# Squares added by VectorE, gate units first, selection rounds gathered in the first attention, layers written out

## The reference, cut to what matters

```python
def swiglu(x, w_gate, w_up, w_down):
    return (jax.nn.silu(x @ w_gate) * (x @ w_up)) @ w_down
...
    x = x + 0.5 * swiglu(rmsnorm(x, ffn1_norm), ffn1_w_gate, ffn1_w_up, ffn1_w_down)
    h = rmsnorm(x, mix_norm) @ w_in
    ...
    o_a = chunk_relpos_attention(hd4(a_q, A_HEADS), hd4(a_k, A_HEADS), hd4(a_v, A_HEADS), a_rel_bias)
    o_b = dsa_attention(rope(hd4(b_q, B_HEADS), pos), rope(hd4(b_k, B_HEADS), pos), hd4(b_v, B_HEADS),
                        rope(hd4(i_q, IDX_HEADS), pos), rope(i_k[:, :, None, :], pos)[:, :, 0, :], i_w)
    o_c = mla_attention(c_q, c_kv, c_kr, c_q_norm, c_kv_norm, c_w_uq, c_w_ukv, pos)
    x = x + jnp.concatenate([o_a, o_b, o_c], axis=-1) @ w_out
    x = x + 0.5 * swiglu(rmsnorm(x, ffn2_norm), ffn2_w_gate, ffn2_w_up, ffn2_w_down)
```

```python
        gates = jax.nn.sigmoid(proj("gates").reshape(b, s, N_BRANCH, D_MODEL) + b_gate[l])
        projected = jnp.einsum('bsnc,ncd->bsnd', branches, w_branch[l])
        mixed = jnp.sum(gates * projected, axis=2)
        x = x + mixed @ w_out[l]
        ...
        x = x + (jax.nn.silu(gate_pre) * val) @ w_down[l]
```

## Time and profile before

| | us |
|---|---|
| median of 3 runs (lowest, highest) | 4180.34 (4179.41, 4185.32) |
| profiled execution, its span | 4181.7, 4180.1 |
| PE busy | 3886.0 (93%) |
| DVE busy | 1864.2 (45%) |
| ACT busy | 1487.7 (36%) |
| POOL busy | 427.1 (10%) |
| granted clock, mean | 0.961 |

### The profile page before, as it was taken

One profiled execution on the slowest core, in us unless ns is written; L12 is line 12 of the kernel. 1 busy time (PEld: TensorE's weight loads), 2 busy tenths in 40 slices (PEclk: granted clock), 3 DMA queues, 4 the chain that ended last, 5 costly groups with the idle time before them and its releaser, 6 DMA issues.

```text
span 4180.1 us, 50030 instructions
## 1 busy us (share of the span) xinstructions
PE 3886.0 (93%) x17196; PEld 3048.2 (73%) x17196; DVE 1864.2 (45%) x3059; ACT 1487.7 (36%) x2433; POOL 427.1 (10%) x414
## 2 busy tenths in 40 slices
PE   7999997789999999987899998899999999898999
PEld 6887664578878887664678886777776668577887
DVE  3433457644434433467544344335542224634652
ACT  3222343432223223333432234436534453523221
POOL 1100001111001100011011021101100000101110
PEclk9999998899999999998899999999999999999999
DMA  3332221023323323211123333131122203222333
GB/s 107 95 98 98 81 61 46 10 82 97 96 91 91 95 95 116 61 43 39 43 85 96 106 116 87 43 84 46 46 76 55 62 22 92 74 80 80 96 92 99
DMA packets 484466, 322.07 MB, mean 77 GB/s; under 512 B 10929, under 2 KB 464177, under 8 KB 483281
## 3 DMA queue, kind: packets, MB, share of 16 engines
q1 hardware_dynamic: 479760, 303.91, 24.8%
q0 software_dynamic: 3392, 14.03, 1.0%
q10 hardware_dynamic: 1152, 2.10, 0.1%
HBM read 310.82 MB, written 8.52 MB: 76 GB/s over the span
## 4 chain that ended last, share of the span: by engine, by line
PE 65%; issue 19%; DVE 5%; ACT 4%; DVEq 3%; POOL 2%; POOLq 2%; ACTq 0%; DMA 0%; SPq 0%
PE bank L233 18%; PE bank L235 18%; PE bank L234 18%; ACT w_hi L218 2%; PE bank L2115 1%; PE bank L2121 1%; DVEq L2427 1%; POOLq L396 1%; PE bank L2135 1%; DVEq L2441 1%; PE bank L2124 1%; DVE s_ring L2432 1%; PE bank L974 1%; PE bank L1172 1%; PE bank L1199 1%
## 5 line engine op out<-in xcount | busy, mean ns | idle before, releaser
L233 PE MATMUL bank<-h_hi,w_hi 128*128 128x512 f32 x3064 | 1234.6, 403 | 63.3 <-DVE h_lo L386 35.5
L225 DVE TENSOR_TENSOR w_lo<-w_raw,w_hi 128x1024 fp32r<-128x1024 f32 (+1 forms) x571 | 741.0, 1299 | 1118.1 <-ACT w_hi L218 1113.4
L235 PE MATMUL bank<-h_lo,w_hi 128*128 128x512 f32 x3128 | 1230.3, 393 | 0.0
L234 PE MATMUL bank<-h_hi,w_lo 128*128 128x512 f32 x3064 | 1205.5, 393 | 0.0
L218 ACT ACTIVATE w_hi<-w_raw 128x1024 fp32r<-128x1024 f32 (+1 forms) x571 | 591.8, 1038 | 581.0 <-DMA w_raw<-in_ffn_w_down 316.0
L233 PEld LDWEIGHTS bank<-h_hi,w_hi 128*128 128x128 f32 x3064 | 580.6, 189 | 232.9 <-issue 47.5
L235 PEld LDWEIGHTS bank<-h_lo,w_hi 128*128 128x128 f32 x3128 | 591.1, 189 | 130.3 <-issue 2.5
L234 PEld LDWEIGHTS bank<-h_hi,w_lo 128*128 128x128 f32 x3064 | 580.5, 189 | 115.1 <-issue 2.7
L233 PE MATMUL bank<-g_hi,w_hi 128*128 (+1 forms) x880 | 342.7, 389 | 2.9 <-DVE gu_ring L2443 2.9
L235 PE MATMUL bank<-g_lo,w_hi 128*128 (+1 forms) x880 | 342.6, 389 | 0.0
L234 PE MATMUL bank<-g_hi,w_lo 128*128 (+1 forms) x880 | 342.6, 389 | 0.0
(11 more groups left out here) (428 smaller groups left out, 4549.7 us busy)
## 6 DMA issues: line engine op xcount, KB each, us to landing
w_raw<-in_w_in SPq DMA_DIRECT2D x105, 512.0 KB, 3.8
w_raw<-in_ffn_w_gate SPq DMA_DIRECT2D x88, 512.0 KB, 3.8
w_raw<-in_ffn_w_up SPq DMA_DIRECT2D x88, 512.0 KB, 3.8
w_raw<-in_ffn_w_down SPq DMA_DIRECT2D x88, 512.0 KB, 3.4
w_raw<-in_w_mix SPq DMA_DIRECT2D x50, 512.0 KB, 4.0
w_raw<-in_w_up SPq DMA_DIRECT2D x44, 512.0 KB, 3.8
w_raw<-in_w_branch SPq DMA_DIRECT2D x32, 512.0 KB, 4.1
w_raw<-in_w_down SPq DMA_DIRECT2D x22, 512.0 KB, 3.4
```

The lines of the kernel that those rows point to most:

```text
L225: dve.tensor_tensor(WL[:, slot(c), 0:w], RAW[:, slot(c), 0:w], WH[:, slot(c), 0:w].bitcast(F32), ALU.subtract).then_inc(w_lo, 1)
L233: pe.matmul(bank, wh, xh, start=start, stop=False)
L234: pe.matmul(bank, wl, xh, start=False, stop=False)
L235: return pe.matmul(bank, wh, xl, start=False, stop=stop)
```

## The change

Four edits. In an FFN, the squares go to eight tiles of their own (`SQUARES`; four of them are tiles of rings that are not yet in use then), DVE adds them instead of POOL, between its two weight splits, ACT splits both weights before the root, and PE runs gate 0, up 0 and half of gate 1 before it needs the sum; the root's matmuls come after gate 1. In a branch stage the order is gate, gate, branch, branch, with the loads and splits in the same order, and PE waits before the second gate for the bank's last reader (`bank_read`). The selection rounds all run in attention A: none in its first four steps, two a step in the next eight, three a step from the twelfth. The loops over the two layers are written out on all five engines.

```diff
+    SQUARES = [XSQ[:, k, :] for k in range(4)] + [SG[:, 0, :], SG[:, 1, :], GU[:, 0, :], GU[:, 1, :]]
...
         for k in range(KT):
-            act.wait_ge(xs_add, f * (KT - 1) + (1 + max(1, k - 3) if k >= 3 else 1))
-            act.activation(XSQ[:, k % 3, :], x_tile(k), ACT.Square).then_inc(xs_sq, 1)
+            act.activation(SQUARES[k], x_tile(k), ACT.Square).then_inc(xs_sq, 1)
...
-    def squares_pool(pool, f):
-        pool.wait_ge(xs_stat, f + 1)
-        pass_wait(pool)
+    def squares_dve(dve, f):
         for k in range(1, KT):
-            pool.wait_ge(xs_sq, f * KT + (k + 1))
-            pool.tensor_tensor(XSQ[:, 3, :], XSQ[:, 0 if k == 1 else 3, :], XSQ[:, k % 3, :], ALU.add
-                               ).then_inc(xs_add, 1)
-            pool.drain()
+            dve.wait_ge(xs_sq, f * KT + (k + 1))
+            last = dve.tensor_tensor(SQUARES[0], SQUARES[0], SQUARES[k], ALU.add)
+            dve.drain()
+        last.then_inc(xs_add, 1)
...
     def ffn_act(act, q, c, f):
         hi(act, q, c + AHEAD)
+        hi(act, q, c + 1 + AHEAD)
         root_act(act, f)
-        hi(act, q, c + 1 + AHEAD)
...
     def ffn_dve(dve, q, c, f):
         lo(dve, q, c + AHEAD)
+        squares_dve(dve, f)
+        lo(dve, q, c + 1 + AHEAD)
         root_dve(dve, f)
-        lo(dve, q, c + 1 + AHEAD)
...
     def ffn_pe(pe, q, c, f):
-        def tile(qq, cc, bank, first=False):
+        def tile(qq, cc, bank, first=False, middle=None):
             split_ready(pe, qq, cc)
             for k in range(KT):
+                if middle and k == KT // 2:
+                    middle(pe, f)
...
-            tile(q + i, c + 2 * t, B[2 * t][:, :], first)
-            if first:
-                squares_pe(pe, f)
+            tile(q + i, c + 2 * t, B[2 * t][:, :], first, squares_pe if second else None)
+            if second:
+                root_pe(pe, f)
             pe.wait_ge(us_done, j + 1)
             tile(q + i, c + 2 * t + 1, B[2 * t + 1][:, :])
-            if first:
-                root_pe(pe, f)
...
-            next_round(rounds, 1 if n >= 4 else 0)
+            next_round(rounds, 0 if n < 4 else 2 if n < 12 else 3)
...
-    def branch_pe(pe, c, b, ready):
+    def branch_pe(pe, c, b, ready, bank_read):
...
             for t in range(2):
-                m = i * 2 + (b * KT + t)
-                pe.wait_ge(sg_done, m + 1)
-                tile(i, c + 2 * t, B[2 * t][:, :], hh, hl)
-                if t == 0:
-                    ready(pe)
+                pe.wait_ge(sg_done, i * 2 + (b * KT + t + 1))
+                if t == 1:
+                    bank_read(pe)
                     pass_wait(pe)
-                pe.wait_ge(mx_done, m + 1)
-                tile(i, c + 2 * t + 1, B[2 * t + 1][:, :], lambda k: YH[:, k, :], lambda k: YL[:, k, :])
+                tile(i, c + t, B[2 * t][:, :], hh, hl)
+            ready(pe)
+            pass_wait(pe)
+            for t in range(2):
+                pe.wait_ge(mx_done, i * 2 + (b * KT + t + 1))
+                tile(i, c + 2 + t, B[2 * t + 1][:, :], lambda k: YH[:, k, :], lambda k: YL[:, k, :])
...
-        branch_pe(pe, C0 + U_BR["lru"], 3, lambda e: e.wait_ge(lyl_done, KT + 2))
+        branch_pe(pe, C0 + U_BR["lru"], 3, lambda e: e.wait_ge(lyl_done, KT + 2),
+                  lambda e: e.wait_ge(lx_done, 4 * N_LRU + 4))
...
-        with pe.Fori(0, LAYERS) as l:
+        for l in range(LAYERS):
             layer_pe(pe, l)
```

More of the change, by code:

```diff
@@ L496, in tile, with pair @@
             last.then_inc(w_used, 1)
-        def pair(i, t, first=False):
+        def pair(i, t):
             j = f * FT + i * 2 + t
+            first, second = isinstance(i, int) and t == 0, isinstance(i, int) and t == 1
             pe.wait_ge(gs_done, j + 1)
-            tile(q + i, c + 2 * t, B[2 * t][:, :], first)
-            if first:
-                squares_pe(pe, f)
+            tile(q + i, c + 2 * t, B[2 * t][:, :], first, squares_pe if second else None)
+            if second:
+                root_pe(pe, f)
             pe.wait_ge(us_done, j + 1)
             tile(q + i, c + 2 * t + 1, B[2 * t + 1][:, :])
-            if first:
-                root_pe(pe, f)
-        pair(0, 0, True)
+        pair(0, 0)
         pair(0, 1)
@@ L2045, in branch_act @@
                                ).then_inc(sg_done, 1)
-                hi(act, i, c + 2 * t + 1 + AHEAD)
+            for t in range(2):
+                hi(act, i, c + 2 + t + AHEAD)
     def branch_dve(dve, c, b, n):
@@ L2051, in branch_dve @@
             for t in range(2):
+                lo(dve, i, c + t + AHEAD)
+            for t in range(2):
                 m = i * 2 + (b * KT + t)
-                lo(dve, i, c + 2 * t + AHEAD)
-                lo(dve, i, c + 2 * t + 1 + AHEAD)
-                dve.wait_ge(w_used, i * RING + (c + 2 * t + 6))
+                lo(dve, i, c + 2 + t + AHEAD)
+                dve.wait_ge(w_used, i * RING + (c + t + 7))
                 dve.wait_ge(sg_done, m + 3)
@@ L2416, in up2_dve @@
         lo(dve, 0, c + AHEAD)
+        squares_dve(dve, f)
+        lo(dve, 0, c + 1 + AHEAD)
         root_dve(dve, f)
-        lo(dve, 0, c + 1 + AHEAD)
         dve.wait_ge(xs_r, f + 1)
@@ L2459, in up2_pe, with tile @@
         hh, hl = h_parts()
-        def tile(i, cc, bank, first=False):
+        def tile(i, cc, bank, first=False, middle=None):
             split_ready(pe, i, cc)
             for k in range(KT):
+                if middle and k == KT // 2:
+                    middle(pe, f)
                 if first:
@@ L2467, in tile, with pair @@
             last.then_inc(w_used, 1)
-        def pair(i, t, first=False):
+        def pair(i, t):
             j = i * 2 + t
+            first, second = isinstance(i, int) and t == 0, isinstance(i, int) and t == 1
             pe.wait_ge(cg_done, j + 1)
-            tile(i, c + 2 * t, B[2 * t][:, :], first)
-            if first:
-                squares_pe(pe, f)
+            tile(i, c + 2 * t, B[2 * t][:, :], first, squares_pe if second else None)
+            if second:
+                root_pe(pe, f)
             pe.wait_ge(us_done, j + (f * FT + 1))
             tile(i, c + 2 * t + 1, B[2 * t + 1][:, :])
-            if first:
-                root_pe(pe, f)
-        pair(0, 0, True)
+        pair(0, 0)
         pair(0, 1)
@@ L2647, in block2_pool @@
         lru_pool(pool)
-        squares_pool(pool, 4)
         ffn_pool(pool, 4)
@@ L2673, in block2_pe @@
               project_pe_parts(pe, 0, C0 + U_FOX0, fox_items0, PF, RF, *h_of, hn0=HF_, banks=WOVEN, thirds=True))
-        branch_pe(pe, C0 + U_BR["mem"], 0, lambda e: e.wait_ge(y_lo, YF + 2))
+        branch_pe(pe, C0 + U_BR["mem"], 0, lambda e: e.wait_ge(y_lo, YF + 2),
+                  lambda e: e.wait_ge(pt_done, SM + 16 + 2))
         def fox_hook(e, n):
@@ L2718, in _ @@
             hi(act, 0, c)
-        with act.Fori(0, LAYERS) as l:
+        for l in range(LAYERS):
             layer_act(act, l)
@@ L2740, in _ @@
             lo(dve, 0, c)
-        with dve.Fori(0, LAYERS) as l:
+        for l in range(LAYERS):
             layer_dve(dve, l)
@@ L2746, in _ @@
     def _(pool):
-        for s, n in ((gl_done, 2), (lyl_done, 2), (xs_add, 1)):
+        for s, n in ((gl_done, 2), (lyl_done, 2)):
             pool.sem_inc(s, n)
@@ L2751, in _ @@
         pool.drain()
-        with pool.Fori(0, LAYERS) as l:
+        for l in range(LAYERS):
             layer_pool(pool, l)
@@ L2757, in _ @@
     def _(pe):
-        for s, n in ((w_used, RING), (nm_stat, 2), (tr_done, 2), (pv_done, 2), (hv_done, 1), (hn_st, 2), (sbv_done, 1), (lr_done, 1), (xs_stat, 1)):
+        for s, n in ((w_used, RING), (nm_stat, 2), (tr_done, 2), (pv_done, 2), (hv_done, 1), (hn_st, 2), (sbv_done, 1), (lr_done, 1)):
             pe.sem_inc(s, n)
```

26 lines of the change are left out of this document (13 added, 13 removed).

## The result

Ten executions of the changed kernel have a median of 4161.1 us (4151.8 to 4174.1), ten of the kernel before 4181.0. The profiled execution is the fastest of the ten, 4151.8 us (span 4149.8), against 4181.7 of the kernel before. PE is busy 3879.5 us of it, DVE 1881.2, ACT 1482.9, POOL 376.0.

The account below looks back on a forecast made before the run. PE, busy 3886.0 of 4180.1 us, was taken to set the time. FFN starts 49.2, LRU branch 3.4 and selection rounds 5.4 sum to 58.0: 4123.7 from the profiled 4181.7, 4122.3 against the median; range 4092 to 4150.

Parts of the forecast that it names:

- FFN starts: Five FFN starts, adds on DVE and gate 1 begun before them: 9.7+10.8+7.9+10.8+10 = 49.2 us won.
- The stall behind the root matmuls: FFN starts: PE waits for the next w_lo on DVE, 1.2 us, and 2.9 at the fifth.
- Recurrence branch: LRU branch: gate 1 goes into PE's wait for branch_lo, 5.45 less 2.0 = 3.4 us won, bounds 0 and 5.5.
- All but the rounds: The forecast gains apart from the selection rounds: FFN starts 49.2 and LRU branch 3.4 us.
- What the rounds give back: C+B start and steps: 5.5 from waits for c_v and w_lo, 12.7 from twelve steps, less 1.5: 16.7 us per layer.
- What they cost in A: Attention A: 30.5 us more DVE rounds per layer, of which 14 show, bounds 4.9 and 30.5.
- the second rival: Attention A: the rounds cost what they last, 33 us less gain in all, 4155; chance 0.15.
- into idle time: Attention A before the twelfth step: one more round a step goes into DVE's idle time.

Follow-up runs that it names:

- e3: The changed kernel with the two layers as a loop on every engine again: 4169.5 us, ratio 0.9967 to the kernel before.
- e7: The changed kernel with the branch stages in their old order (gate, branch, gate, branch): 4161.3 us.
- e1: The changed kernel with the old schedule of selection rounds (one a step of attention A from step 4, 20 in A): 4132.2 us, ratio 0.9871 to the kernel before.
- e6: The changed kernel with its new order on PE, but the squares added by POOL as before: 4174.2 us, ratio 0.9974 to the kernel before.

## Why the prediction was wrong

**FFN starts, 49.2 forecast.** From landmarks (the first h_lo of each FFN, the update of x behind it) the five gained 8.6, 10.3, 7.8 (with the start before the third), 10.6 and 6.0: 43.3. Each of the first four is within 1.1 of its term. The stall behind the root matmuls was priced 1.2 and 2.9 and measured 1.20 and 2.99, and the adds on DVE were in time. The fifth was short by 4: its stall threw PE to the lower clock (0.79 at 3802.33), some 1.5 us which the sum left out, and the same happens once more before the down matmuls, where PE waits 3.37 us and the next matmul lasts 0.79, against 2.93 and 0.50 in the kernel before. The third FFN's start was the loop, as said (e3).

**Recurrence branch, 3.4 forecast.** 1.1 against e7, 4.1 against the kernel before: the size is right, the premise that gate 1 would find its bank free is not (it waits 4.03).

**All but the rounds, 52.6 forecast:** e1 measured 53 between the medians and 49.4 between the spans of the profiled executions. The agreement is in part luck: the FFN starts and the branch gave some 46 at their places, and what the rest is no run here shows.

**What the rounds give back, 16.7 a layer:** 21.5, of which 8.8 are in the C items (5.5 forecast; they also run at full clock now, 1.00 for 0.85) and 12.7 in C+B (12.7 less 1.5 forecast). The 5.5 were put down to the wrong waits. Against the kernel before the C items won 7.2: the wait for c_v went from 4.3 to 2.0 only, the one for w_lo stayed (1.16, now 1.21), and three waits before L805 for t_ring, 4.9 us together, went, which the sum hadn't named.

**What they cost in A: this step failed.** "I take 14, bounds 4.9 and 30.5" should have been 30.9; the second rival's price, the upper bound, was the right one. That its 4155 lies between the profiled 4151.8 and the median is in part luck, since the FFN starts were short by 6 and the rounds gave back 10 more than it had. Read from the starts of A's steps in the first layer, changed kernel against e1: 6.8 us come in steps 4 to 7, "into idle time" as I had put it. There a second round stands ahead of the row maximum, and with it ACT's exp, ACT's reading of the index scores and PE come later, while DVE's idle time lies behind those scores. 4.7 of the 6.8 are slower matmuls, at a clock of 0.89; in the second layer of the same trace, where the clock stays at 1.00, these steps cost 2.1. Steps 8 to 16 cost some 2.5, and from 17 on it is 21.6 where the sum had 15.2 less a little. The windows from step 17 to A's end, changed kernel and e1:

```profile
599.16:684.46 85.30, 54.85 (x220) 40.83 (x219) 61.43 (x130) 25.71 (x52) 7.11 (x8) 0.80 0.10 27
```

```profile
587.00:650.75 63.75, 51.38 (x219) 37.34 (x219) 41.23 (x94) 24.11 (x47) 6.89 (x8) 0.83 0.14 36
```

DVE works 20.2 us more and the stretch is 21.6 longer: the rounds are paid one for one, and nothing is absorbed. 3.5 of the 21.6 are slower matmuls. With the 4.7 of steps 4 to 7 that makes nearly all of the 8.3 of A, a term that the sum didn't have. And I had read one step (620) as level and then still granted the steps around it slack.

The second error was not to ask which rounds cost anything where they were. In the C items twelve of them ran beside PE at full clock (the earlier trace rows show only the two waits at their end); the table says that 28 of the 48 have room in A, and that moving more trades one wait for another.

## What to carry to other kernels

Work on an engine at 45% is free only in steps whose chain does not pass behind it: price a moved instruction by the wait of the critical engine in that very step, step by step, and take the one-for-one price where there is no slack. Move only what costs something where it is, and spread it by measured step starts. A new wait on TensorE can cost more than it lasts, since the clock may fall behind it (some 1.5 us behind the wait of 2.99, 11 behind one of 1.62), and it makes the times scatter.

## What the runs showed of the hardware

Two executions of the same program with the same waits (1.80 and 1.81, 1.63 and 1.62 us) went on at 1.00 in one and at 0.73, then 0.59 in the other: the same work took 25.1 us in the first and 36.5 in the second. Over ten executions the changed kernel scattered by 22 us, with mean clocks from 0.958 to 0.966, and the time fell, by and large, as the clock rose.

A VectorE instruction with two inputs in SBUF (h_lo, 128x512) lasted 0.74 us alone and 1.76 to 1.80 beside POOL's adds (e6).
